# A two-layer hybrid trunk with eight experts: gate and up of the last third in one unit, and one activation table for logarithm and exponential

## The chip, the core and the metric

The kernel runs on one core of a Trainium2 chip. The metric is the device time of one execution in microseconds; lower is better. The core has five engines with queues of their own: TensorE (PE: matrix products, with its weight loads PEld beside them), VectorE (DVE), ScalarE (ACT), GpSimd (POOL) and SyncE (SP, which here only issues DMAs). They meet at semaphores: an instruction waits until a counter has reached a value, and each engine works strictly in the order in which its program is written.

## The reference

One inference step over 256 prompt tokens and 64 sample tokens (8 sequences of 8), width 1024. Layer 0 is a mixer of retention and mLSTM heads and a dense SwiGLU; layer 1 is the HGRN2 recurrence and a layer of eight experts of which each token takes two. The two parts that the change touches, cut to what is computed:

```python
def _hgrn2(q, k, log_f, v, S):              # 8 heads, in chunks; A = cumulative sum of log_f
    inter = einsum(qc * exp(A), S)
    dec   = exp(where(causal, A[t] - A[s], -inf))
    s     = einsum(qc, dec * kc)
    S_new = exp(A_end) * S + einsum(kc * exp(A_end - A), vc)
...
def _moe(h, ...):
    for e in range(8):
        out += gates[e] * (silu(h @ wg[e]) * (h @ wu[e])) @ wd[e]    # wg, wu: 1024x2816, wd: 2816x1024
```

f = lower + (1 - lower) * sigmoid(...), k = 1 - f, log_f = log(f), q = silu(...), all in float32.

## The kernel before, in words

**Products in three parts.** Every float32 weight is split into a high part (fp32r, written by ACT: `w_hi` L1716, `dense_hi` L1374) and a low part (the rest, written by DVE: `w_lo` L2361, `dense_lo` L1878). A product is three matmuls, high by high, low by high and high by low (`product3`, L509 to L511).

**The expert loop** (from 740 us of the span to its end) has eight rounds of one expert here, with up to 128 tokens each (`expert_round`). The 2816 hidden columns are taken in three chunks, c = 0, 1, 2, of 1024, 1024 and 768 columns. A round has 35 units of weights, in the order of `UNITS`: gate 0, up 0, gate 1, up 1, down 0, gate 2, up 2, down 1, down 2. A unit of gate or up holds two k-tiles of 128 rows (2x1024 columns, or 2x768 in chunk 2), one of down two rows of tiles. SP loads a unit into one of seven stages as soon as DVE has split what lay there (`load_unit`, L1279 and L1287); ACT and DVE split it into one of four slots as soon as PE has used what lay there (`SLOT_OF`, `ahead`). So PE is followed by ACT, ACT by DVE and DVE by SP, each at a fixed distance. A PSUM bank holds 512 columns: gate goes to banks 0 and 1, up to banks 2 and 3, and with 768 columns the second bank of each pair is half used: its matmuls have 256 columns. After the last unit of gate, ACT takes silu of it (`silu`, L1757); after the last unit of up, DVE multiplies (`product`, L2461); PE turns the result two units later (`turn`, L1151), and down needs it turned. `spread` (L1090) gathers the tokens of the next expert through banks 0 and 1.

The last round differs: at unit 20 DVE computes gates and slots first (`gates_and_last_slots`, L2433 to L2449), and the end of it is joined with the final norm.

**The third block** (HGRN2, 486 to 690 us) is an order written out by hand, `C_STEPS`, in which every engine picks the steps that concern it. Heads 0 to 3 are the first group (steps with a), heads 4 to 7 the second (b). f, q, g, v are tiles of the input projection on PE (L509 to L511), scaled to SBUF by DVE (L2290) or, for v, by ACT (L1662). sig, forget, ln make the forget gate on ACT (L1667, L1625/L1628, L1672), scan is its cumulative sum on DVE (L2297/L2298). For each of eight levels, da/db are differences on DVE (L2227/L2229), xa/xb their exponentials on ACT (L1634/L1637 for level 7, L1642, L1644), pa/pb products on DVE (L2237/L2238 for level 7, L2241/L2243), la/lb products on PE (L987, level 7 L982, the diagonal L966) that DVE takes over (L2258). wh and wl split the next dense unit (ACT L1374, DVE L1878). silu1 is silu of q of heads 4 to 7 (L1675). end, xend and kend (DVE L2323, ACT L1687 to L1690, DVE L2329) make the keys for the new state, which PE turns (turn, L720). ACT holds one table of functions at a time; where the next function is not in it, an ACT_TABLE_LOAD stands ahead of it.

Of the kernel before, what the change touches and what calls it, by code (L numbers as in the profile page):

```python
# [15 lines left out]
P = 128  # L16
# [55 lines left out]
    q4 sig1 pa5 forget4 la5 q5 forget5 xa6 la6 wh forget6 forget7 pa6 ln1 da7 scan1 xa7 q6 q7 wl la7 pa7 silu1 end0  # L72
    xend0 kend0 v0 xb0 v1 pb0 wh db1 wh xb1 wl lb0 turn0 lb1 v2 la8 v3 db2 pb1 v4 wl wh xb2 wl out0 v5 v6 pb2
# [97 lines left out]
def trunk_kernel(nc, A, O):  # L171
    with ExitStack() as ctx:
# [122 lines left out]
        part_units = lambda kind, c: [(kind, c, q) for q in range(CHW[c] // 256 if kind == "d" else KD // 2)]  # L295
        UNITS = [u for kind, c in (("g", 0), ("u", 0), ("g", 1), ("u", 1), ("d", 0), ("g", 2), ("u", 2), ("d", 1), ("d", 2))
# [4 lines left out]
        gate_end = {turn_of[("g", c, KD // 2 - 1)]: c for c in range(NCH)}  # L301
        up_end = {turn_of[("u", c, KD // 2 - 1)]: c for c in range(NCH)}
# [172 lines left out]
        def _(pe):  # L475
# [652 lines left out]
            def expert_round(it, last):  # L1128
# [18 lines left out]

                def turn(c):
# [47 lines left out]
                for p, (kind, c, q) in enumerate(UNITS):  # L1196
                    if kind == "d" and c == 2 and last:
                        if q == 0:
                            last_down()
                    elif kind == "d":  # L1200
                        down(c, q)
                    else:
                        gate_or_up(kind, c, q)
# [21 lines left out]
        def _(sp):  # L1225
# [44 lines left out]
            def load_unit(e, p):  # L1270
# [9 lines left out]
                else:  # L1280
                    n = CHW[c]
                    v = stage[:, 0:2 * n].rearrange("p (k n) -> p k n", n=n)
                    for j in range(2):
                        k = 2 * q + j
                        src = (wg if kind == "g" else wu)[:, bass.ds(e, 1), k:k + 1, c * CH:c * CH + n].rearrange(
# [48 lines left out]
        def _(act):  # L1334
# [295 lines left out]
            def level_exps(s, j):  # L1630
                act.wait_ge(S(f"level_diff{s}"), 8 - j)
                L = LV[s][j % 2]
                if j == 7:
                    fn(L[:, :, L_SECOND], CUM[:, 4 * s:4 * s + 4, P:TP], ACT.Exp)  # L1634
# [11 lines left out]
            for name, u in C_STEPS:  # L1646
# [18 lines left out]
                elif name == "sig":  # L1665
                    after_empty(act, ("c", "f", 7))
                    fn(K[:, 4:8, :], K[:, 4:8, :], ACT.Sigmoid).then_inc(S("f_sigmoid"), 1)  # L1667
                elif name == "forget":
# [170 lines left out]
        def _(dve):  # L1839
# [392 lines left out]
            def level_products(s, j):  # L2232
                L, at = LV[s][j % 2], slice(4 * s, 4 * s + 4)
                dve.wait_ge(S("hgrn_k"), 4 * s + 4)
                dve.wait_ge(S(f"level_exp{s}"), 8 - j)
                if j == 7:
                    v.tensor_tensor(L[:, :, L_SECOND], L[:, :, L_SECOND], Q[:, at, P:TP], ALU.mult)  # L2237
                    v.tensor_tensor(L[:, :, L_FIRST], L[:, :, L_FIRST], K[:, at, 0:P], ALU.mult).then_inc(S(f"level_mul{s}"), 1)  # L2238
# [45 lines left out]
            for name, u in C_STEPS:  # L2284
# [41 lines left out]
                elif name == "kend":  # L2326
                    at = slice(4 * u, 4 * u + 4)
                    dve.wait_ge(S("end_exp"), 2 * u + 2)
                    v.tensor_tensor(K[:, at, :], K[:, at, :], LV[u][1][:, :, :], ALU.mult).then_inc(S("hgrn_kend"), 1)  # L2329
# [121 lines left out]
            def expert_round(it, last):  # L2451

                def product(c):
# [6 lines left out]
                    for g, at in bank_columns(c):  # L2460
# [233 lines left out]
```

## Time and profile before

| what | us |
|---|---|
| median of three runs | 1516.8 (1511.55 to 1517.97) |
| the profiled execution | 1510.73 |
| its span, first to last instruction | 1508.9 |
| PE busy | 1479.9 (98%) |
| DVE busy | 1157.2 (77%) |
| ACT busy | 936.5 (62%) |
| the expert loop, from 740 to the end | 769 |

The span is what the trace covers; the 1.8 us beside it lie outside its first and last instruction. Busy time of PE counts matmuls that overlap (one of 512 columns is shown with 390 ns, and the next starts 227 ns after it), so PE's pace is read from the distance of starts, and its idle time from the bracket behind a row.

### The profile page before, as it was taken

What the parts mean: (1) busy time and instruction counts of PE and PEld (TensorE: products, weight loads), DVE (VectorE), ACT (ScalarE), POOL (GpSimd) and SP (SyncE); (2) the same over time, 40 slices, a digit from 0 to 9 for tenths busy, and PEclk for the clock granted to TensorE, in tenths of its full rate; (3) what the DMA queues carried; (4) which work ended last, traced back from release to release, by engine and by line L of the source; (5) the groups of instructions that cost most, each with busy time, mean ns of one, the idle gap of its engine ahead of it and who ended that gap; (6) DMA issues with size and microseconds to landing.
All of it is one profiled execution on the core that took longest, in us unless ns stands there. A gap on an engine that the chain in (4) does not pass through costs nothing.

```text
span 1508.9 us, 23251 instructions
## 1 busy us (share of the span) xinstructions
PE 1479.9 (98%) x8573; PEld 1312.6 (87%) x8573; DVE 1157.2 (77%) x1306; ACT 936.5 (62%) x975; POOL 88.3 (6%) x96
## 2 busy tenths in 40 slices
PE   9999999999999989999999999999999999999997
PEld 8899888999999979989788888888888888888885
DVE  5756677555455697777798888988889888898897
ACT  5434555334333774354777877778777787777875
POOL 1023110000000000120300000000000000000011
PEclk9999999999999999999999999999999999999999
DMA  8577724997445523451999999999999999999994
GB/s 250 134 136 139 138 88 135 284 296 208 123 145 175 159 84 114 144 159 60 362 406 381 389 362 394 378 377 385 363 393 380 377 389 358 391 379 379 395 334 170
DMA packets 213588, 404.03 MB, mean 268 GB/s; under 512 B 13471, under 2 KB 130491, under 8 KB 213390
## 3 DMA queue, kind: packets, MB, share of 16 engines
q1 hardware_dynamic: 202976, 372.82, 71.0%
q0 software_dynamic: 6320, 22.20, 4.9%
q10 hardware_dynamic: 4222, 8.05, 1.4%
q8 instruction: 47, 0.77, 0.2%
q14 instruction: 23, 0.19, 0.0%
HBM read 372.74 MB, written 30.28 MB: 267 GB/s over the span
## 4 chain that ended last, share of the span: by engine, by line
PE 87%; DVE 6%; ACT 3%; DMA 2%; issue 1%; POOL 0%; SPq 0%; DVEq 0%; ACTq 0%; POOLq 0%
PE bank L509 26%; PE bank L510 25%; PE bank L511 25%; PE bank L733 1%; DVE dense_lo L1878 1%; PE bank L1151 1%; DMA arena<-in_w_moe_down 1%; PE bank L775 1%; PE bank L678 1%; DVE w_lo L2361 1%; DVE arena L2007 1%; PE bank L725 1%; ACT dense_hi L1374 0%; PE bank L987 0%; PE bank L1100 0%
## 5 line engine op out<-in xcount | busy, mean ns | idle before, releaser
L2361 DVE TENSOR_TENSOR w_lo<-arena,w_hi 128x2048 fp32r<-128x2048 f32 (+1 forms) x280 | 596.9, 2165 | 87.1 <-ACT w_hi L1716 85.9
L1716 ACT ACTIVATE w_hi<-arena 128x2048 fp32r<-128x2048 f32 (+1 forms) x280 | 501.2, 1819 | 119.7 <-PE bank L511 114.2
L509 PE MATMUL bank<-w_hi,xg_hi 128*128 128x512 f32 (+1 forms) x768 | 287.3, 374 | 0.3
L510 PE MATMUL bank<-w_lo,xg_hi 128*128 128x512 f32 (+1 forms) x768 | 286.1, 373 | 0.0
L511 PE MATMUL bank<-w_hi,xg_lo 128*128 128x512 f32 (+1 forms) x768 | 285.4, 372 | 0.0
L1878 DVE TENSOR_TENSOR dense_lo<-ring,dense_hi 128x2048 fp32r<-128x2048 f32 (+1 forms) x78 | 167.8, 2151 | 122.0 <-ACT dense_hi L1374 121.9
L1374 ACT ACTIVATE dense_hi<-ring 128x2048 fp32r<-128x2048 f32 (+1 forms) x78 | 140.5, 1802 | 139.9 <-PE bank L511 114.7
L509 PEld LDWEIGHTS bank<-w_hi,xg_hi 128*128 128x128 f32 x768 | 144.5, 188 | 29.0 <-issue 3.1
L511 PEld LDWEIGHTS bank<-w_hi,xg_lo 128*128 128x128 f32 x768 | 144.2, 188 | 25.8
L510 PEld LDWEIGHTS bank<-w_lo,xg_hi 128*128 128x128 f32 x768 | 144.5, 188 | 24.9
L509 PE MATMUL bank<-h_hi,dense_hi 128*128 128x320 f32 x448 | 143.3, 320 | 3.9 <-DVE h_lo_a L1891 1.4
L509 PE MATMUL bank<-w_hi,at_hi 128*128 128x512 f32 x352 | 139.5, 396 | 0.2 <-DVE w_lo L2361 0.2
L511 PE MATMUL bank<-h_hi,dense_lo 128*128 128x320 f32 x448 | 139.3, 311 | 0.0
L511 PE MATMUL bank<-w_hi,at_lo 128*128 128x512 f32 x352 | 137.3, 390 | 0.0
L510 PE MATMUL bank<-w_lo,at_hi 128*128 128x512 f32 x352 | 137.0, 389 | 0.0
L509 PE MATMUL bank<-h_hi_f,dense_hi 128*128 128x320 f32 x352 | 109.0, 310 | 0.0
L510 PE MATMUL bank<-h_lo_f,dense_hi 128*128 128x320 f32 x352 | 108.8, 309 | 0.0
L511 PE MATMUL bank<-h_hi_f,dense_lo 128*128 128x320 f32 x352 | 108.8, 309 | 0.0
L509 PEld LDWEIGHTS bank<-h_hi,dense_hi 128*128 128x128 f32 x448 | 85.2, 190 | 8.0 <-DVE dense_lo L1878 3.2
L511 PEld LDWEIGHTS bank<-h_hi,dense_lo 128*128 128x128 f32 x448 | 85.0, 190 | 0.0
L510 PE MATMUL bank<-h_lo_a,dense_hi 128*128 128x320 f32 x256 | 79.3, 310 | 0.0
L511 PEld LDWEIGHTS bank<-w_hi,at_lo 128*128 128x128 f32 x352 | 66.1, 188 | 14.1
(458 smaller groups left out, 2383.2 us busy)
## 6 DMA issues: line engine op xcount, KB each, us to landing
arena<-in_w_moe_down SPq DMA_DIRECT2D x176, 512.0 KB, 6.7
arena<-in_w_moe_gate SPq DMA_DIRECT2D x128, 512.0 KB, 7.0
arena<-in_w_moe_up SPq DMA_DIRECT2D x128, 512.0 KB, 7.2
arena<-in_w_moe_gate SPq DMA_DIRECT2D x64, 384.0 KB, 5.7
arena<-in_w_moe_up SPq DMA_DIRECT2D x64, 384.0 KB, 4.1
ring<-in_w_in_ab SPq DMA_DIRECT2D x32, 512.0 KB, 9.2
ring<-in_w_in_c SPq DMA_DIRECT2D x32, 512.0 KB, 4.7
expert_rows<-ZERO SPq DMA_DIRECT2D x12, 1024.0 KB, 7.7
```

The costliest lines, as they stand in the source:

```text
L509: mm(out, left[0], right[0], start=start, stop=False)
L510: mm(out, left[0], right[1], start=False, stop=False)
L511: return mm(out, left[1], right[0], start=False, stop=stop)
L678: mm(banks[3][:, 0:256], ZERO[:, 0:P], ZERO[:, :], start=True, stop=True)
L725: mm(b[:, 0:TP], left(0), probs[:, 0:TP], start=True, stop=False, skip_group_check=True)
L733: ins = mm(b[:, TP + s * TS:TP + (s + 1) * TS], states[:, s, :], right[:, s * TS:(s + 1) * TS], start=False, stop=(s == NB - 1), skip_grou ...
L775: ins = mm(b[:, h * 256:(h + 1) * 256].rearrange("p (b v) -> p b v", v=DH), kn[rows_g, 2, :], VX[rows_g, at, :], start=True, stop=True)
L1151: ins = nc.tensor.transpose(banks[6 + j // 4][:, j % 4 * P:(j % 4 + 1) * P], AN[:, j * P:(j + 1) * P], ident)
L1374: fn(unit_flat(n, DWH), unit_flat(n, DST), ACT.Copy).then_inc(S("dense_hi"), 1)
L1716: fn(WH[SLOT_OF[p]][:, 0:unit_size(p)], STAGE[:, s, 0:unit_size(p)], ACT.Copy).then_inc(S("unit_hi"), 1)
L1878: v.tensor_tensor(unit_flat(n, DWL), unit_flat(n, DST), unit_flat(n, DWH).bitcast(F32), ALU.subtract).then_inc(S("dense_split"), 1)
L2361: v.tensor_tensor(WL[w][:, 0:n], STAGE[:, s, 0:n], WH[w][:, 0:n].bitcast(F32), ALU.subtract).then_inc(S("unit_split"), 1)
```

## The change

**In the expert loop**, chunk 2 has eight units of kind "gu" in place of four of gate and four of up: each holds one k-tile of gate (768 columns) and the same of up (768), side by side, 1536 columns as before. PE multiplies the 1536 columns in three pieces of 512, into banks 0, 1 and 2; bank 1 so holds the last 256 columns of gate and the first 256 of up. silu of chunk 2 comes after the last of these units instead of after the fourth, and DVE's product reads up from the second half of bank 1 and from bank 2. SP loads gate and up in turns.

**In the third block**, the table that holds both logarithm and exponential is asked for ahead of xa0 and behind sig1; level 7 signals after its first exponential as well, and DVE starts the first of its two products then. The steps at the first group's end stand in another order, end0 ahead of pa7, xb0 ahead of xend0 and pb0 ahead of kend0.

```diff
-    q4 sig1 pa5 forget4 la5 q5 forget5 xa6 la6 wh forget6 forget7 pa6 ln1 da7 scan1 xa7 q6 q7 wl la7 pa7 silu1 end0
-    xend0 kend0 v0 xb0 v1 pb0 wh db1 wh xb1 wl lb0 turn0 lb1 v2 la8 v3 db2 pb1 v4 wl wh xb2 wl out0 v5 v6 pb2
+    q4 sig1 pa5 forget4 la5 q5 forget5 xa6 la6 wh forget6 forget7 pa6 ln1 da7 scan1 xa7 q6 q7 wl la7 end0 silu1 xb0 pa7 pb0
+    xend0 kend0 v0 v1 wh db1 wh xb1 wl lb0 turn0 lb1 v2 la8 v3 db2 pb1 v4 wl wh xb2 wl out0 v5 v6 pb2
...
-        part_units = lambda kind, c: [(kind, c, q) for q in range(CHW[c] // 256 if kind == "d" else KD // 2)]
-        UNITS = [u for kind, c in (("g", 0), ("u", 0), ("g", 1), ("u", 1), ("d", 0), ("g", 2), ("u", 2), ("d", 1), ("d", 2))
+        part_units = lambda kind, c: [(kind, c, q) for q in range({"d": CHW[c] // 256, "gu": KD}.get(kind, KD // 2))]
+        UNITS = [u for kind, c in (("g", 0), ("u", 0), ("g", 1), ("u", 1), ("d", 0), ("gu", 2), ("d", 1), ("d", 2))
...
+                def gate_and_up(q):
+                    p = turn_of[("gu", 2, q)]
+                    pe.wait_ge(S("unit_split"), it * NU + p + 1)
+                    if q == 0:
+                        pe.wait_ge(S("silu_done"), it * NCH + 2)
+                        pe.wait_ge(S("a_ready"), it * NCH + 2)
+                    for g in range(3):
+                        at = slice(g * 512, (g + 1) * 512)
+                        ins = product3(banks[g][:, :], (XGH[:, q, :], XGL[:, q, :]),
+                                       [w[SLOT_OF[p]][:, at] for w in (WH, WL)], q == 0, q == KD - 1)
+                    ins.then_inc(S("unit_used"), 1)
...
-                        k = 2 * q + j
-                        src = (wg if kind == "g" else wu)[:, bass.ds(e, 1), k:k + 1, c * CH:c * CH + n].rearrange(
+                        k = q if kind == "gu" else 2 * q + j
+                        src = ((wg, wu)[j] if kind == "gu" else wg if kind == "g" else wu)[:, bass.ds(e, 1), k:k + 1, c * CH:c * CH + n].rearrange(
...
                 if j == 7:
-                    fn(L[:, :, L_SECOND], CUM[:, 4 * s:4 * s + 4, P:TP], ACT.Exp)
+                    if s == 0:
+                        nc.scalar.preload_act_table_set("natural_log_exp_and_others")
+                    fn(L[:, :, L_SECOND], CUM[:, 4 * s:4 * s + 4, P:TP], ACT.Exp).then_inc(S(f"level_exp{s}"), 1)
...
                     fn(K[:, 4:8, :], K[:, 4:8, :], ACT.Sigmoid).then_inc(S("f_sigmoid"), 1)
+                    nc.scalar.preload_act_table_set("natural_log_exp_and_others")
...
-                dve.wait_ge(S(f"level_exp{s}"), 8 - j)
+                dve.wait_ge(S(f"level_exp{s}"), 1 if j == 7 else 9 - j)
                 if j == 7:
                     v.tensor_tensor(L[:, :, L_SECOND], L[:, :, L_SECOND], Q[:, at, P:TP], ALU.mult)
+                    dve.wait_ge(S(f"level_exp{s}"), 2)
...
                     dve.wait_ge(S("end_exp"), 2 * u + 2)
+                    dve.wait_ge(S(f"level_mul{u}"), 8)
...
-                    for g, at in bank_columns(c):
-                        ins = v.tensor_tensor(AN[:, at], SL[:, at], banks[2 + g][:, 0:at.stop - at.start], ALU.mult)
+                    if c < 2:
+                        ups = [(at, banks[2 + g][:, 0:at.stop - at.start]) for g, at in bank_columns(c)]
+                    else:
+                        ups = [(slice(0, 256), banks[1][:, 256:512]), (slice(256, 768), banks[2][:, :])]
+                    for at, up in ups:
+                        ins = v.tensor_tensor(AN[:, at], SL[:, at], up, ALU.mult)
```

PE's program in the expert loop, first k-tiles of chunk 2 (w_hi_62 and w_lo_66 are parts of one slot of the weights, xg_hi and xg_lo the tokens; one bank of 512 columns is filled by three rows). Before:

```order
L509 MATMUL bank<-w_hi_62,xg_hi 128x512
L510 MATMUL bank<-w_lo_66,xg_hi 128x512
L511 MATMUL bank<-w_hi_62,xg_lo 128x512
L509 MATMUL bank<-w_hi_62,xg_hi 128x256
L510 MATMUL bank<-w_lo_66,xg_hi 128x256
L511 MATMUL bank<-w_hi_62,xg_lo 128x256
```

and in the changed kernel:

```order
L1150 REGISTER_ALU
L509 MATMUL bank<-w_hi_62,xg_hi 128x512
L510 MATMUL bank<-w_lo_66,xg_hi 128x512
L511 MATMUL bank<-w_hi_62,xg_lo 128x512
L509 MATMUL bank<-w_hi_62,xg_hi 128x512
L510 MATMUL bank<-w_lo_66,xg_hi 128x512
L511 MATMUL bank<-w_hi_62,xg_lo 128x512
```

The six rows before stand 16 times in a round (96 matmuls); in the changed kernel a k-tile of gate and up together has nine of 512 columns, 72 in a round.

ACT's program in the third block, from ln1 on. L1672 is the logarithm, L1644 xa7, L1675 silu1, L1687 the start of xend0. Before:

```order
L1672 ACT_TABLE_LOAD
L1672 ACTIVATE arena<-arena 128x1280
L1644 ACT_TABLE_LOAD
L1644 ACTIVATE arena<-arena 128x1280
L1675 ACT_TABLE_LOAD
L1675 ACTIVATE arena<-arena 128x1280
L1687 ACT_TABLE_LOAD
L1687 ACTIVATE arena<-arena,TOTAL 128x128
```

and in the changed kernel, where the same functions have the lines L1689, L1660, L1692 and L1704 and xb0 has L1650 and L1653:

```order
L1689 ACTIVATE arena<-arena 128x1280
L1660 ACTIVATE arena<-arena 128x1280
L1692 ACT_TABLE_LOAD
L1692 ACTIVATE arena<-arena 128x1280
L1650 ACT_TABLE_LOAD
L1650 ACTIVATE arena<-arena 128x4x128
L1653 ACTIVATE arena<-arena 128x128 x4
L1704 ACTIVATE arena<-arena,TOTAL 128x128
```

The loads ahead of the logarithm and of xa7 are gone (one that stood ahead of xa6 now stands right behind sig1), and xb0 is done ahead of xend0.

ACT's program in the expert loop at the end of chunk 2 (the register instructions between are the loop's counters). Before, silu of chunk 2 (L1757) stands two splits behind the start of up; in the changed kernel (L1774) it stands behind the split of unit 30:

```order
L1733 ACTIVATE w_hi_64<-arena 128x2048
L1768 REGISTER_ALU
L1774 ACTIVATE arena<-bank 128x512
L1774 ACTIVATE arena<-bank 128x256
L1732 REGISTER_ALU
L1733 ACTIVATE w_hi_62<-arena 128x2048
```

## Rows read from the trace of the kernel before

**Rows 1.** Busy time by stretch: us, PE, PEld, DVE, ACT, POOL, clock, DMA share, GB/s.

```profile
836.00:932.00 96.00, 95.98 (x461) 80.26 (x460) 82.80 (x50) 74.37 (x55) 0.00 (x0) 1.00 0.99 382
```

**Rows 2.** Waits of PE, 480 to 740 us: in total, times, longest.

```profile
PE bank L987 <- DVE arena L2243: 4.0, 3, 1.6
```

**Rows 3.** Waits of PE, 740 to 1508 us.

```profile
PE bank L509 <- DVE w_lo L2361: 0.2, 1, 0.2
```

**Rows 4.** Waits of the DMA queue, 836 to 1412 us.

```profile
SPq L1287 <- DVE w_lo L2361: 245.0, 141, 3.5
```

**Rows 5.** Timeline of PE, round 2: start, us, row, [idle before <-releaser].

```profile
862.49 0.48 PE L509 MATMUL bank<-w_hi,xg_hi 128*128 128x512 f32 x1
...
878.90 0.39 PE L509 MATMUL bank<-w_hi,at_hi 128*128 128x512 f32 x1
...
890.71 0.39 PE L509 MATMUL bank<-w_hi,xg_hi 128*128 128x512 f32 x1
...
906.09 0.28 PE L509 MATMUL bank<-w_hi,xg_hi 128*128 128x256 f32 x1
...
906.44 0.40 PE L509 MATMUL bank<-w_hi,xg_hi 128*128 128x512 f32 x1
...
907.49 0.40 PE L509 MATMUL bank<-w_hi,at_hi 128*128 128x512 f32 x1
```

**Rows 6.** Timelines around the end of chunk 2; the last row from round 8.

```profile
909.99 1.01 DVE L2461 TENSOR_TENSOR arena<-arena,bank 128x512 f32<-128x512 f32 x2
...
910.43 3.72 ACT L1716 ACTIVATE w_hi<-arena 128x2048 fp32r<-128x2048 f32 x2 [2.92 <-PE bank L511]
...
912.96 0.81 PE L1151 MATMUL bank<-cst,arena 128*128 128x128 f32 x6
...
1463.08 0.87 ACT L1757 ACTIVATE arena<-bank 128x512 f32<-128x512 f32 x2 [0.60 <-PE bank L511]
```

**Rows 7.** Last round: DVE's timeline, the chain's DMA, PE's timeline.

```profile
1461.33 13.37 DVE L2361 TENSOR_TENSOR w_lo<-arena,w_hi 128x1536 fp32r<-128x1536 f32 x7
...
1468.78 15.45 DMA arena<-in_w_moe_down
...
1488.62 0.50 PE L509 MATMUL bank<-w_hi,at_hi 128*128 128x512 f32 x1 [0.17 <-DVE w_lo L2361]
```

**Rows 8.** Timelines of ACT, DVE and PE at level 7 of the first group.

```profile
523.37 1.26 ACT L1637 ACTIVATE arena<-arena 128x128 f32<-128x128 f32 x4
...
524.76 0.69 DVE L2237 TENSOR_TENSOR arena<-arena 128x512 f32<-128x512 f32 x1 [1.44 <-ACT arena L1637]
...
526.11 1.16 PE L982 MATMUL bank<-arena 128*128 128x128 f32 x8 [0.93 <-DVE arena L2238]
```

**Rows 9.** Timelines of ACT, DVE and PE around the first group's end.

```profile
556.48 1.28 ACT L1672 ACT_TABLE_LOAD   x1
557.77 1.27 ACT L1672 ACTIVATE arena<-arena 128x1280 f32<-128x1280 f32 x1
...
557.37 0.88 DVE L2229 TENSOR_TENSOR arena<-arena 128x256 f32<-128x256 f32 x2
...
559.08 0.56 DVE L2297 TENSOR_TENSOR_SCAN arena<-cst,arena 128x192 f32<-128x192 f32 x1 [0.84 <-ACT arena L1672]
...
565.50 0.39 PE L509 MATMUL bank<-dense_hi,h_hi 128*128 128x256 f32 x1 [2.39 <-DVE dense_lo L1878]
...
568.43 0.40 ACT L1687 ACTIVATE arena<-arena,TOTAL 128x128 f32<-128x128 f32 x1 [2.58 <-DVE arena L2323]
...
571.52 1.49 DVE L2329 TENSOR_TENSOR arena<-arena 128x1280 f32<-128x1280 f32 x1 [3.13 <-ACT cst L1690]
...
575.33 0.55 PE L720 MATMUL bank<-cst,arena 128*128 128x128 f32 x3
```

**Rows 10.** Busy time by stretch, columns as in rows 1.

```profile
540.00:543.00 3.00, 2.12 (x16) 2.12 (x17) 3.00 (x11) 0.84 (x2) 0.00 (x0) 1.00 0.01 2
...
566.00:570.00 4.00, 4.00 (x24) 4.00 (x23) 2.39 (x8) 1.57 (x6) 0.00 (x0) 0.57 0.80 266
```

More of the change, by code:

```diff
@@ L300, in trunk_kernel @@
         turn_of = {u: p for p, u in enumerate(UNITS)}
-        gate_end = {turn_of[("g", c, KD // 2 - 1)]: c for c in range(NCH)}
-        up_end = {turn_of[("u", c, KD // 2 - 1)]: c for c in range(NCH)}
+        gate_end = {turn_of[("g", c, KD // 2 - 1) if c < 2 else ("gu", 2, KD - 1)]: c for c in range(NCH)}
+        up_end = {turn_of[("u", c, KD // 2 - 1) if c < 2 else ("gu", 2, KD - 1)]: c for c in range(NCH)}
         gate_last, up_last = {c: p for p, c in gate_end.items()}, {c: p for p, c in up_end.items()}
@@ L1201, in expert_round @@
                         down(c, q)
+                    elif kind == "gu":
+                        gate_and_up(q)
                     else:
```

## The prediction

> **What bounds the kernel now.** I read the busy times by stretch first, then who waited for whom, then the timelines where the change sits. In the expert loop PE is busy 95.98 of 96 us at a clock of 1.00 [rows 1], and from 740 us on it waits for weights once, 0.2 us [rows 3]. The DMA engines look full as well, 0.99 [rows 1], but their queue waited 245 us in 576 for DVE to free a stage [rows 4], for one of its two lines alone: transfers follow PE, not the other way round. So a round ends when PE has got through its matmuls. The last round is different (below). In the third block PE does wait: 4.0 us for DVE's level products [rows 2] and 2.39 us at 565.50 for the low part of a dense unit [rows 9]. Those waits lie on the path, since PE has nothing else queued that could run.
>
> **The loop.** The row to compare is chunk 2, 890.71 to 907.49: 16.78 us for 96 matmuls [rows 5]. One k-tile of gate or of up is 906.44 to 907.49, 1.05 us, three matmuls of 512 columns and three of 256. The three of 256 take 906.09 to 906.44, 0.35 us; so the three of 512 take 0.70 us, 0.233 each. The changed stretch is 72 matmuls of 512 columns. A stretch of just that is in the same round, 862.49 to 878.90: 16.41 us [rows 5], 0.228 each. The saving is 16.78 - 16.41 = 0.37 us a round. From one side it is bounded by the case that the 512s keep 0.233: 72 x 0.233 = 16.8, nothing saved. From the other: the stretch of 16.41 starts behind transposes and its first row is 0.48 us long instead of the usual 0.39 [rows 5]; without that 0.09 us it is 16.32, and the saving 0.46. I take 0.37, since that is the same instruction in the same number.
>
> The Trainium skill ("TensorE: Matmul & The Clock Gate", Back-to-back issue gap) has a lone matmul's gap at its columns over 2.4 GHz plus about 2.5 ns. By that rule, as an estimate, 24 fewer matmuls save 24 x 2.5 ns = 0.06 us a round. The trace has 0.117 us for 256 columns and 0.228 for 512 and no such constant; I follow the trace, and keep the rule's outcome as a rival.
>
> The saving counts in seven rounds, not eight. In the last round DVE splits seven units back to back from 1461.33 for 13.37 us, behind its work on gates and slots; the last unit's transfer is issued at 1468.78 off that chain, lands 15.45 us later, and PE waits for its low part at 1488.62 [rows 7]. That chain starts from units before chunk 2, so PE reaches the wait earlier and waits longer. 7 x 0.37 = 2.6 us.
>
> What hides the rest: silu of chunk 2 moves behind the eighth unit. PE ends that at 907.49, and ACT sat idle for 2.92 us until 910.43 there [rows 6]; silu of 768 columns takes 0.87 (the row of round 8). DVE starts its product at 909.99, which was later than PE because it still split, and PE turns at 912.96. silu done at about 908.6 is ahead of 909.99, so the product doesn't move; its cover is 912.96 - 911.00 = 1.96 us, of which the faster PE takes 0.37 at most. Queued behind silu on ACT are the splits of units 31 and 32, which wait for PE until 910.43 anyway. The moved loads are as many, of the same size and in the same stages, and the bytes are the same; only their order changes. The required rate rises by 0.4%. I cost both at nothing.
>
> **The third block, level 7.** ACT's single exponential of the second half ends as the four others start, 523.37; they last 1.26; DVE idled 1.44 us until 524.76 and then did two products, and PE had waited 0.93 us at 526.11 [rows 8]. Now the first product (0.69) runs beside the four exponentials, and only the second lies behind them: PE starts some 0.6 us earlier, and so does everything on DVE, which has no gap from there to the differences that feed xa5 and whose chain then runs over ACT. I take 0.6; bounds are 0 (a tile of PE becomes late in that stretch, where its clock is low for a while) and 0.69.
>
> **ln1 and xa7.** The load at 556.48 lasts 1.28; the logarithm follows at 557.77, and DVE, free at 557.37 + 0.88 = 558.25, waits 0.84 us for it until 559.08 [rows 9]. The load that stood ahead of xa6 still costs its 1.28 in the same gap, only earlier. Without the load of ln1, the logarithm ends at 557.77 and is no longer late; DVE's differences are what is late next, so the scan gains 0.84 and not 1.28. Then come the scan, q6, q7 and the split for v0, in an unbroken row on DVE, and PE's wait of 2.39 us before 565.50 [rows 9] ends 0.8 us earlier. With the 0.6, PE starts v0 at 564.1. The second load removed, ahead of xa7, lies beside DVE's scan: nothing.
>
> In the new order xend0 waits for xb0. Before, ACT was ready for xend0 2.58 us ahead of 568.43 [rows 9], at 565.85; silu1 and its loads ahead of that follow q7 on DVE, so they come 1.4 us earlier, 564.4. xb0 takes 1.26 for its four exponentials [rows 8] and some 0.5 for the one before them: xend0 starts at 566.2 instead of 568.43, and kend0 at 571.52 - 2.2 = 569.3, for 1.49 us. PE wants it for turn0, 575.33 - 565.50 = 9.8 us behind v0's start: at 573.9, or 572.3 if the clock stays up. Cover at the least 572.3 - 570.8 = 1.5 us. DVE idled 3.13 us ahead of kend0 [rows 9]; of that the earlier start takes 0.8 and pb0's two products (0.69 each, [rows 8]) 1.4. No new wait.
>
> **The clock.** Behind the 2.39 us gap PE's granted clock was 0.57 on average from 566 to 570, that is, mostly at 1.2 instead of 2.4 GHz [rows 10], which costs 4 x 0.43 = 1.7 us, all of it on PE's path. Behind a gap of near 0.9 us within 540 to 543 the clock stayed at 1.00 [rows 10], and PE's longest wait for L2243 was 1.6 us [rows 2]. The new gap is 2.39 - 0.8 = 1.6 us. Whether the clock falls after it can't be told from one trace; I take it that it does not, with 6 in 10, and count 0 to 1.7.
>
> **The sum.** Loop 2.6, level 7 0.6, ln1 0.8, clock 1.7: 5.7 us; 4.0 if the clock still falls. Against the profiled execution, 1510.73 (span 1508.9 and 1.8 beside it), that is 1505.0. The runs shown have a median of 1516.8, 6.1 above the profiled one; carried over to it, 1516.8 - 5.7 = 1511.1. The runs spread over 6.4 us (1511.55 to 1517.97), more than the change, so a median of the changed kernel can fall at either side of that: 1506 or 1512.
>
> **Rivals.**
> 1. The clock falls as before, and the rest holds: 4.0 us, 1512.8. For it: the gap only shrinks, it doesn't go. Against it: the gap of 1.6 us.
> 2. The loop gives nothing, because the 512s keep 0.233 or because the gap is as the rule has it; the block gives 1.4 and perhaps 1.7: 1516.8 - 1.4 to 3.1, 1514. For it: the wide 512s in rows 5. Against it: no other stretch of only 512s runs at 0.233.
> 3. PE gets more than I count: 0.46 in eight rounds (3.7), and the waits for L2243 shrink too, since ACT is 1.3 us freer. 3.7 + 1.4 + 1.7 + 1.5 = 8.3: 1508.5.
> 4. Slower. The product of chunk 2 comes late. Its cover is 1.96 us [rows 6]; if silu misses ACT's idle 2.92 us and falls behind the next two splits (3.72 us, from 910.43), it ends at 915.0 and the product at 916.0, 3.1 us behind the turn. In seven rounds 21 us, less the 5.7: 1532. It decides from the point where silu ends later than about 912. Against it: in ACT's program silu stands ahead of those splits.
>
> That the table change does nothing is excluded by ACT's program: the two loads are gone from it.
>
> **How the numbers follow.** Forecast 0.50, rival 1 0.22, rival 2 0.13, rival 3 0.11, rival 4 0.04. A difference under 0.5% (7.6 us) can't be told from none here. Faster by more is rival 3 and those cases of the forecast and of rival 1 in which the median falls among the lower runs, 0.11 + 0.20: 0.31. Slower by more is rival 4: 0.04. The rest, 0.65, is within. The range: low from 1506 less a margin for rival 3, 1504.5; high from rival 2 with the spread of a median, 1516.5. It leaves out rival 4 and the outer parts of 2 and 3.
>
> **What would show it.** Right: chunk 2 of rounds 1 to 7 takes 16.4 us, the last unit's wait in round 8 grows by about 0.4, and PE waits for no product; PE's wait before v0 is 1.6 us, the one at level 7's product 0.3, the clock stays at 1.00 behind v0's start; ACT has no load between xa6 and silu1. Wrong: 16.8 us in chunk 2, a bracket on PE's L1163 (turn) or on its L720, or a span that falls by more than 7 us.

## The result and the profile after

| | before | after |
|---|---|---|
| first comparison, median (lowest to highest), 5 runs each | 1516.27 (1511.55 to 1517.97) | 1503.42 (1500.85 to 1505.5) |
| ratio, 95% interval | | 0.9932 (0.9905 to 0.9958) |
| second comparison, later runs (experiment 1), 12 and 7 runs | 1510.05 (1508.61 to 1518.96) | 1504.06 (1501.99 to 1504.5) |
| ratio, 95% interval | | 0.9954 (0.9937 to 0.9972) |
| profiled execution (span) | 1510.73 (1508.9) | 1504.12 (1502.3) |

The changed kernel is faster. 1503.42 lies 7.7 us under the forecast of 1511.1 and 1.1 under the low end of the range. The two profiles lie 6.6 us apart and the second comparison 6.0; the forecast difference was 5.7. So the change is worth about 6 us, and what failed is how it was carried over to a median (the section on why the prediction was right and wrong). A ratio is estimated over all runs of a comparison and differs a little from the quotient of the two medians.

The lines of the changed kernel (the run "after"): chunk 2 of gate and up is L509 to L511 as before, turn is L1163, the splits are L1733 (high) and L2380 (low), silu L1774, product L2484. In the block the logarithm is L1689, the scan L2315, silu1 L1692, xend L1704, kend L2348, the low part of a dense unit L1895, level products L2254 to L2261.

Expert loop: PE's timeline in round 2 of after, to be read against [rows 5]:

```profile
859.49 0.48 PE L509 MATMUL bank<-w_hi,xg_hi 128*128 128x512 f32 x1
...
875.91 0.39 PE L509 MATMUL bank<-w_hi,at_hi 128*128 128x512 f32 x1
...
887.72 0.39 PE L509 MATMUL bank<-w_hi,xg_hi 128*128 128x512 f32 x1
...
904.04 0.39 PE L509 MATMUL bank<-w_hi,at_hi 128*128 128x512 f32 x1
```

Chunk 2 takes 904.04 - 887.72 = 16.32 us (16.78 before), the stretch that I took as its model still 16.42. All rounds 1 to 7 together took 657.53 us and now take 654.20. Around the end of chunk 2, against [rows 6]:

```profile
904.24 0.87 ACT L1774 ACTIVATE arena<-bank 128x512 f32<-128x512 f32 x2
906.68 1.01 DVE L2484 TENSOR_TENSOR arena<-arena,bank 128x256 f32<-128x256 f32 x2
906.96 3.72 ACT L1733 ACTIVATE w_hi<-arena 128x2048 fp32r<-128x2048 f32 x2 [1.85 <-PE bank L511]
...
909.48 0.82 PE L1163 MATMUL bank<-cst,arena 128*128 128x128 f32 x6
```

silu sits in ACT's gap (2.92 us of idle time became 1.85), ends at 905.1, and the product still ends 1.8 us before PE's turn, which has no bracket. PE's waits from 737 us of after to the end, against [rows 3]:

```profile
PE bank L1121 <- ACT last_hi L1844: 1.2, 1, 1.2
PE bank L509 <- DVE w_lo L2380: 0.3, 1, 0.3
```

The first is in the tail (before has it too), the second in the last round, right behind DVE's work on gates.

Third block, level 7 of the first group (ACT, DVE, PE), against [rows 8]:

```profile
522.19 1.26 ACT L1653 ACTIVATE arena<-arena 128x128 f32<-128x128 f32 x4
522.41 0.69 DVE L2254 TENSOR_TENSOR arena<-arena 128x512 f32<-128x512 f32 x1 [0.28 <-ACT arena L1650]
...
523.48 0.69 DVE L2256 TENSOR_TENSOR arena<-arena 128x512 f32<-128x512 f32 x1 [0.38 <-ACT arena L1653]
...
524.23 0.94 PE L982 MATMUL bank<-arena 128*128 128x128 f32 x6 [0.23 <-DVE arena L2256]
```

DVE's first product now runs beside the four exponentials, and PE waits 0.23 us instead of 0.93. From the logarithm to turn0, in order of time, against [rows 9]:

```profile
554.48 1.28 ACT L1689 ACTIVATE arena<-arena 128x1280 f32<-128x1280 f32 x1
...
556.30 0.54 DVE L2315 TENSOR_TENSOR_SCAN arena<-cst,arena 128x192 f32<-128x192 f32 x1
...
560.48 1.27 ACT L1692 ACTIVATE arena<-arena 128x1280 f32<-128x1280 f32 x1 [1.50 <-DVE arena L2308]
...
562.70 0.39 PE L509 MATMUL bank<-dense_hi,h_hi 128*128 128x256 f32 x1 [1.47 <-DVE dense_lo L1895]
...
564.77 0.39 ACT L1704 ACTIVATE arena<-arena,TOTAL 128x128 f32<-128x128 f32 x1
...
567.85 1.49 DVE L2348 TENSOR_TENSOR arena<-arena 128x1280 f32<-128x1280 f32 x1 [1.05 <-ACT cst L1707]
...
571.04 0.55 PE L720 MATMUL bank<-cst,arena 128*128 128x128 f32 x3
```

The scan has no bracket (0.84 before), PE's wait ahead of v0 is 1.47 (2.39 before), kend ends 1.7 us before turn0, and turn0 waits for nothing. The granted clock behind v0 and later in the block (the third number from the end of a row), against [rows 10]:

```profile
562.00:566.00 4.00, 3.30 (x27) 3.30 (x28) 4.00 (x10) 3.99 (x11) 0.00 (x0) 1.00 0.54 169
566.00:570.00 4.00, 4.00 (x36) 4.00 (x35) 2.94 (x6) 3.36 (x10) 0.00 (x0) 1.00 0.29 98
656.00:663.00 7.00, 7.00 (x25) 3.90 (x26) 5.37 (x11) 3.62 (x7) 2.12 (x3) 0.51 0.60 204
```

Behind v0 it stays at the upper level, 2.4 GHz, where before had 0.57 for 4 us. But from 656 to 663 us it is at the lower level of 1.2 GHz, with PE busy all the time before (36.00 of 36 us from 620 to 656) and in it; in the same stretch before had 1.00. Where the 6.6 us between the two profiles went, by distances of starts on PE:

| stretch | before | after | change |
|---|---|---|---|
| start to level 7's first product, without its wait | 525.18 | 524.00 | -1.2, unchanged code |
| PE's wait at that product | 0.93 | 0.23 | -0.7 |
| that product to v0 | 39.39 | 38.47 | -0.9 |
| v0 to the loop | 174.92 | 175.20 | +0.3 |
| rounds 1 to 7 | 657.53 | 654.20 | -3.3 |
| last round, to the last product with the gathered rows | 100.77 | 100.04 | -0.7 |
| from there to the end | 10.18 | 10.16 | 0.0 |

The first line isn't the change's: before has a clock fall at 208 to 211 us (0.50 there) that after doesn't have, in code that is the same. Without that line 5.4 us are left. The second pair of profiles (before_again, 1507.45, and after_again, 1503.67) lies only 3.8 us apart, because there the unchanged stretch ahead of level 7 is 1.9 us longer in the changed kernel; without it 5.7 are left.

### The profile page after: what moved, and what is told of

Read it like the earlier page. It is cut to its first block, busy times and chain, and to the rows that moved or that the text cites. A ratio compares the mean times of both kernels' runs of the same rounds, so it can differ in the third digit from the quotient of the medians.

```text
span 1502.3 us, 22859 instructions
## 1 busy us (share of the span) xinstructions
PE 1475.0 (98%) x8381; PEld 1300.3 (87%) x8381; DVE 1156.2 (77%) x1306; ACT 935.7 (62%) x973; POOL 89.5 (6%) x96
## 4 chain that ended last, share of the span: by engine, by line
PE 91%; DVE 7%; ACT 2%; issue 1%; POOL 0%; DVEq 0%; ACTq 0%; POOLq 0%
PE bank L509 27%; PE bank L511 26%; PE bank L510 26%; PE bank L733 2%; DVE dense_lo L1895 1%; PE bank L1163 1%; PE bank L775 1%; PE bank L678 1%; PE bank L657 1%; PE bank L987 1%; PE bank L725 1%; PE bank L1100 0%; PE bank L666 0%; PE bank L1090 0%; DVE arena L2024 0%
## 5 line engine op out<-in xcount | busy, mean ns | idle before, releaser
L2380 DVE TENSOR_TENSOR w_lo<-arena,w_hi 128x2048 fp32r<-128x2048 f32 (+1 forms) x280 | 596.9, 2165 | 82.1 <-ACT w_hi L1733 80.0
L1733 ACT ACTIVATE w_hi<-arena 128x2048 fp32r<-128x2048 f32 (+1 forms) x280 | 502.0, 1820 | 117.0 <-PE bank L511 111.1
L509 PE MATMUL bank<-w_hi,xg_hi 128*128 128x512 f32 x704 | 275.6, 392 | 0.5 <-DVE w_lo L2380 0.3
L511 PE MATMUL bank<-w_hi,xg_lo 128*128 128x512 f32 x704 | 274.1, 389 | 0.0
L510 PE MATMUL bank<-w_lo,xg_hi 128*128 128x512 f32 x704 | 273.9, 389 | 0.0
L1895 DVE TENSOR_TENSOR dense_lo<-ring,dense_hi 128x2048 fp32r<-128x2048 f32 (+1 forms) x78 | 167.8, 2151 | 122.5 <-ACT dense_hi L1388 122.3
L509 PEld LDWEIGHTS bank<-w_hi,xg_hi 128*128 128x128 f32 x704 | 132.1, 188 | 30.7 <-issue 3.1
L511 PEld LDWEIGHTS bank<-w_hi,xg_lo 128*128 128x128 f32 x704 | 132.1, 188 | 27.7
L510 PEld LDWEIGHTS bank<-w_lo,xg_hi 128*128 128x128 f32 x704 | 132.2, 188 | 27.0
L509 PE MATMUL bank<-h_hi,dense_hi 128*128 128x320 f32 x448 | 142.2, 317 | 3.9 <-DVE h_lo_a L1908 1.4
L509 PE MATMUL bank<-w_hi,at_hi 128*128 128x512 f32 x352 | 139.3, 396 | 0.0
L511 PE MATMUL bank<-h_hi,dense_lo 128*128 128x320 f32 x448 | 138.3, 309 | 0.0
L511 PE MATMUL bank<-w_hi,at_lo 128*128 128x512 f32 x352 | 137.3, 390 | 0.0
L509 PE MATMUL bank<-h_hi_f,dense_hi 128*128 128x320 f32 x352 | 109.0, 310 | 0.0
L511 PE MATMUL bank<-h_hi_f,dense_lo 128*128 128x320 f32 x352 | 108.8, 309 | 0.0
L509 PEld LDWEIGHTS bank<-h_hi,dense_hi 128*128 128x128 f32 x448 | 84.2, 188 | 8.0 <-DVE dense_lo L1895 3.2
L511 PEld LDWEIGHTS bank<-h_hi,dense_lo 128*128 128x128 f32 x448 | 84.1, 188 | 0.0
L511 PEld LDWEIGHTS bank<-w_hi,at_lo 128*128 128x128 f32 x352 | 66.1, 188 | 14.0
```

What stands on the lines that cost most here:

```text
L509: mm(out, left[0], right[0], start=start, stop=False)
L510: mm(out, left[0], right[1], start=False, stop=False)
L511: return mm(out, left[1], right[0], start=False, stop=stop)
L1733: fn(WH[SLOT_OF[p]][:, 0:unit_size(p)], STAGE[:, s, 0:unit_size(p)], ACT.Copy).then_inc(S("unit_hi"), 1)
L1895: v.tensor_tensor(unit_flat(n, DWL), unit_flat(n, DST), unit_flat(n, DWH).bitcast(F32), ALU.subtract).then_inc(S("dense_split"), 1)
L2380: v.tensor_tensor(WL[w][:, 0:n], STAGE[:, s, 0:n], WH[w][:, 0:n].bitcast(F32), ALU.subtract).then_inc(S("unit_split"), 1)
```

## The experiments

**1. How far do two copies of one kernel lie apart?** No edit.

> An unchanged copy of the kernel before, for a second profile and to see how far two of its medians lie apart. The plain runs of before and after lie 12.8 us apart in their medians, the two profiles 6.6. Theory A (two levels of the kernel before: its runs lie near 1512 or near 1517, by how often TensorE's clock falls): the runs of this copy fall near both levels, the ratio's interval holds 1, and a run at 1517 has a mean clock lower by about 0.003 than one at 1512. Theory B (it waits for DMAs in some runs): the clock is the same in long and short runs, and the profile shows other waits of PE for transfers. In the last round PE's first matmul on the last unit of down waits 0.17 us for its low part again if that wait belongs to the schedule; with a transfer of another length than 15.45 us it is chance.

1508.52 us (11 runs) beside 1510.17 (35 runs of the kernel before), ratio 0.9992 (0.9981 to 1.0003). Theory A holds in part: long runs exist, but they are rare. Of 47 runs of the kernel before in this study's two timed comparisons, 42 lie between 1507.7 and 1511.8 and 5 between 1515.0 and 1520.7; none of the copy's 11 is of the long kind. Three of the five long runs have a mean clock of 0.988 to 0.990, below all others (0.992 to 0.996); the other two, at 0.992 and 0.993, can't be told from them by the clock. In the first comparison 3 of 5 were of the long kind. The last round shows what was chance in the profile of before. Its last down transfer was issued at 1468.78 us, and ACT began to split it at 1484.33, 15.55 us later; in before_again the issue was at 1466.01 and the split began 12.64 us later, in after at 1462.92 and 13.82 us later. The rows of the split, in this order:

```profile
1484.33 1.91 ACT L1716 ACTIVATE w_hi<-arena 128x2048 fp32r<-128x2048 f32 x1 [3.13 <-DMA arena<-in_w_moe_down]
```

```profile
1478.65 1.92 ACT L1716 ACTIVATE w_hi<-arena 128x2048 fp32r<-128x2048 f32 x1 [0.57 <-DMA arena<-in_w_moe_down]
```

```profile
1476.73 1.91 ACT L1733 ACTIVATE w_hi<-arena 128x2048 fp32r<-128x2048 f32 x1 [1.95 <-DMA arena<-in_w_moe_down]
```

In the 14 profiles this distance is 11.8 to 14.0 us, but for before (15.55) and tables_again (18.29, below). The 18 matmuls around the wait of [rows 7] (1485.45 to 1490.12 us of before) take 4.67 us there and 4.18 to 4.20 in all other profiles but tables_again.

> An unchanged copy of the changed kernel, timed beside runs of the kernel before on the same chip. In the first comparison the medians lay 12.8 us apart; alone, the loop's part gave 2.9 us and the block's part 2.7 us against one and the same set of runs. Theory A (the parts add, and the first comparison met a slow group of the kernel before): 1504 to 1505 against 1510, a difference of 5 to 6 us, ratio 0.9965. Theory B (both together give more than their sum): 10 us or more, ratio 0.993 again. In the trace: level 7's first product to v0 takes 38.5 us, rounds 93.49 us, the last round 100.0 us to the last down matmul, and the clock is at 1.00 behind v0.

1504.06 against 1510.05, ratio 0.9954 (0.9937 to 0.9972). Theory A: the difference is 6.0 us. The trace has 38.48 us from level 7 to v0, 654.18 for seven rounds, 100.36 for the last round (the wait behind the gates was 0.58 us here).

**2. Each half alone.** loop_only has the change's edits of the expert loop (the units of kind "gu" and what follows from them) and the third block as before. block_only has the edits of the third block (both preloads, level 7's early signal, the order of the steps with kend's wait) and the loop as before.

> Only the change in the expert loop (units of gate and up together in chunk 2), the third block as before. My theory: the loop's part is 7 times 0.46 us plus what the last round gives, 3.3 to 4.1 us, and chunk 2 takes 16.3 us; nothing changes ahead of the loop. So about 1511 to 1512 against a kernel before at 1515, ratio 0.9975. Rival (the two parts help each other, or the loop's part is worth more in plain runs than in the profile): 8 us or more. Rival (the gain came with the block's other clock phase): chunk 2 at 16.8.

1507.30 against 1510.17 (-2.9), ratio 0.9989 (0.9974 to 1.0004); chunk 2 16.32 us, seven rounds 654.26, last round 100.06. The interval holds 1 (two of its 12 runs are of the long kind), so it's the rows of the trace that show the loop's part, not the runs.

> Only the change in the third block, the loop as before. My theory: 0.7 us at level 7, 0.9 us ahead of v0, and the clock behind v0 stays at 1.00, 1.5 us, which a clock fall later can give back: 1.6 to 3.1 us, ratio 0.9985. Chunk 2 takes 16.78 us. Rival (the clock): the plain runs gain more than 5 us, because the kernel before loses more to clock falls in its runs than in its profile, and the mean clock listed with the runs is higher by 0.002 or more than that of the runs before.

1507.46 (-2.7), ratio 0.9987 (0.9978 to 0.9996); level 7's wait 0.23, 38.46 us to v0, seven rounds 657.55. -2.9 and -2.7 add up to -5.6, and both together gave -6.0: the halves add up as far as the runs can tell, and neither holds a hidden 10 us.

**3. Widths or units?**

```diff
-                    for g in range(3):
-                        at = slice(g * 512, (g + 1) * 512)
+                    for g, (a0, a1) in enumerate(((0, 512), (512, 768), (768, 1280), (1280, 1536))):
```

> The loop's change as in loop_only (eight units of gate and up together, silu behind the last, same loads), but each k-tile is multiplied in pieces of 512, 256, 512 and 256 columns as before, 96 matmuls in chunk 2. If the gain comes from the widths alone, chunk 2 takes 16.78 us and the kernel is the same as before (ratio 1.000). If it comes from the units' order, the loads' order or silu's place, chunk 2 takes 16.3 us and the ratio is 0.9975.

1510.75, ratio 1.0007 (0.9989 to 1.0026). PE's timeline, first and last row of chunk 2 and the first of down: 908.05 - 891.27 = 16.78 us. Seven rounds take 657.55 us (657.53 before), the last 100.31.

```profile
891.27 0.39 PE L509 MATMUL bank<-w_hi,xg_hi 128*128 128x512 f32 x1
...
907.93 0.28 PE L511 MATMUL bank<-w_hi,xg_lo 128*128 128x256 f32 x1
908.05 0.40 PE L509 MATMUL bank<-w_hi,at_hi 128*128 128x512 f32 x1
```

The loop's gain is the widths of PE's matmuls; units, loads and silu's place are worth nothing either way in the trace (by the runs alone, nothing to within 4 us). Then the same columns in six pieces of 256 (`for g in range(6)` over 256 columns each):

> As loop_only, but the 1536 columns of a k-tile are multiplied in six pieces of 256: 144 matmuls in chunk 2 instead of 72. Theory of a fixed cost for each matmul (24 fewer saved 0.46 us, so 19 ns each, and 256 columns cost 0.123 us): 144 x 0.123 = 17.7 us for chunk 2. Theory of the change of width (256 columns cost 0.1167 us as their three rows in the trace show, and it is a 512 next to a 256 that costs 0.233 instead of 0.227): 144 x 0.1167 = 16.8 us.

One profile. Its chunk 2 begins and ends like this:

```profile
888.93 0.28 PE L1159 MATMUL bank<-w_hi,xg_hi 128*128 128x256 f32 x1
889.05 0.28 PE L1160 MATMUL bank<-w_lo,xg_hi 128*128 128x256 f32 x1
...
906.09 0.28 PE L1161 MATMUL bank<-w_hi,xg_lo 128*128 128x256 f32 x1
906.21 0.40 PE L509 MATMUL bank<-w_hi,at_hi 128*128 128x512 f32 x1
```

17.28 us for 144, 0.120 each: between the two theories, so both were half right. 512 columns cost 16.32 / 72 = 0.2267 us, 256 cost 0.1200: the second 256 columns add 0.1067 us, which is their number over 2.4 GHz, and 13 ns are left for each matmul at either width. A third width checks it. Two rows of after's dense tiles of 320 columns, 15 matmuls apart:

```profile
527.71 0.31 PE L511 MATMUL bank<-h_hi,dense_lo 128*128 128x320 f32 x1
...
529.91 0.31 PE L511 MATMUL bank<-h_hi,dense_lo 128*128 128x320 f32 x1
```

2.20 / 15 = 0.1467 us, and 320 / 2.4 GHz + 13 ns is 0.1463. So 24 fewer matmuls save 24 x 13 ns = 0.32 us of the 0.46. The other 0.14 come with the change of width: 48 x 0.2267 + 48 x 0.1200 = 16.64, and the mixed stretch takes 16.78.

The 13 ns are measured with weights of 128 columns and aren't a constant of every such matmul. after_again has matmuls of 256 columns with weights of 64 columns and, right behind them, with 128 (first and last row of each):

```profile
586.15 0.28 PE L511 MATMUL bank<-dense_hi,h_lo_c 128*64 128x256 f32 x1
...
588.54 0.28 PE L511 MATMUL bank<-dense_hi,h_lo_c 128*64 128x256 f32 x1
...
588.89 0.28 PE L511 MATMUL bank<-dense_hi,h_lo_c 128*128 128x256 f32 x1
...
591.29 0.28 PE L510 MATMUL bank<-dense_lo,h_hi 128*128 128x256 f32 x1
```

2.39 us for 21 is 0.1138 each, 7 ns beside the columns; 2.40 for 20 is 0.1200 again. Matmuls of 320 columns with weights of 36 (level7_only, L511 at 35.96 to L511 at 39.00 us) are 3.04 us for 21, 0.1448 each, 11 ns. What sets this cost isn't shown.

**4. The block's three edits, one at a time.** tables_only has the two preloads alone:

```diff
+                    if s == 0:
+                        nc.scalar.preload_act_table_set("natural_log_exp_and_others")
...
+                    nc.scalar.preload_act_table_set("natural_log_exp_and_others")
```

> The kernel before with one edit: the table with logarithm and exponential is asked for ahead of xa0 and behind sig1. Level 7 and the order of the steps stay. My theory: the scan no longer waits 0.84 us for the logarithm, PE's wait ahead of v0 is 2.39 - 0.84 = 1.55 us and the clock stays at 1.00 from there on; PE's wait at level 7 stays at 0.93. Rival (DVE was late anyway): the wait ahead of v0 stays near 2.4 and the clock falls.

Level 7 to v0 took 38.47 us (39.39 to 39.41 in six profiles without the tables; loop_only, below, aside), PE's wait there 1.47, no clock fall behind. The run as a whole took 1518.04, and its windows show why:

```profile
113.00:131.00 18.00, 16.58 (x71) 15.40 (x71) 5.93 (x14) 3.15 (x9) 1.55 (x3) 0.53 0.44 96
```

18 us at a mean clock of 0.53, in code that no kernel here changes: up to 8.5 us lost (18 x 0.47). It is the one long run that was profiled.

> A second profile of tables_only, whose first one had a clock fall of 17 us at 114 to 131 us, far ahead of the block. My theory: that fall is chance and is gone, level 7's first product is at 524 to 526 us instead of 533.6; its distance to v0 is 38.5 us again, with a wait of 1.47 us and a clock of 1.00 behind it. From v0 to the loop's start 173.6 us if no clock fall follows, 175 to 176 if one does near 660 us. Rival (the fall at 114 belongs to this kernel): it is there again.

The early fall is gone (level 7 at 523.97); 38.45 us to v0 again. This run has two other things. Its last down transfer took 18.19 us to land (by the chain of work that ended last), PE waited 2.9 us for it, and the last round took 105.18 us, so a late last transfer, as in [rows 7], isn't bound to one execution (tables_again has the loop of before; no profile of the changed loop has one). And PE waited at the second group's level 7, as it did in tables_only (0.62):

```profile
571.94 1.16 PE L982 MATMUL bank<-arena 128*128 128x128 f32 x8 [0.63 <-DVE arena L2241]
```

The same row of after, where xb0 and pb0 come ahead of xend0 and kend0, has no bracket:

```profile
571.43 1.06 PE L982 MATMUL bank<-arena 128*128 128x128 f32 x8
```

Level 7's early signal alone:

```diff
-                    fn(L[:, :, L_SECOND], CUM[:, 4 * s:4 * s + 4, P:TP], ACT.Exp)
+                    fn(L[:, :, L_SECOND], CUM[:, 4 * s:4 * s + 4, P:TP], ACT.Exp).then_inc(S(f"level_exp{s}"), 1)
...
-                dve.wait_ge(S(f"level_exp{s}"), 8 - j)
+                dve.wait_ge(S(f"level_exp{s}"), 1 if j == 7 else 9 - j)
...
+                    dve.wait_ge(S(f"level_exp{s}"), 2)
```

> The kernel before with one edit: level 7 signals after its first exponential, and DVE starts its first product then. My theory: PE's wait at its first product of level 7 falls from 0.93 to about 0.25 us; the wait ahead of v0 stays at 2.4 us and the clock falls behind it to about 0.57. Rival: a later tile of PE takes the 0.7 us up, and the distance from the start of the block to v0 doesn't change.

The first theory in each number: 0.23 us at level 7, then 39.41 us to v0 with its wait of 2.40, and a clock fall behind it.

The order alone (the two changed lines of `C_STEPS` and kend's wait for the level products):

> The kernel before with one edit: end0 ahead of pa7, xb0 ahead of xend0, pb0 ahead of kend0, and no change of tables or signals. My theory: it gives nothing, since no PE wait hangs on it: the wait ahead of v0 stays at 2.4 us, the clock falls as before, and the distance from v0 to the loop's start stays near 175 us. Rival (xb0 earlier lets lb0 and what follows start earlier, or pa7 later delays la7): PE's waits between la7 and lb1 change by more than 0.3 us.

Nothing: 39.40 us to v0, wait 2.39, clock fall behind it, 174.81 to the loop. What the order is for shows where the clock stays up behind v0. In the six profiles with the fall there, PE comes late to level 7 of the second group, and pb0 is in time in either order. Where the fall is missing, the three profiles with the old order have PE wait 0.62 to 0.63 us (tables_only, tables_again, and loop_only, whose wait ahead of v0 is the long one, 2.41 us), and the five with the new order don't have it wait. The wait is the same with and without the tables, so it's the clock that makes PE early, and then the old order takes 0.6 us back. The row of loop_only:

```profile
575.50 1.16 PE L982 MATMUL bank<-arena 128*128 128x128 f32 x8 [0.63 <-DVE arena L2252]
```

**5. Is the clock behind v0 a gain?**

> A second profile of block_only, for the clock behind v0. With the wait of 1.47 us ahead of v0 the three profiles so far had no clock fall there, with the wait of 2.4 us six of seven had one. If the clock's part is a real gain, v0 to the loop's start is 173.6 us again, about 1.3 us below the mean of the kernels with the long wait (174.9). If it is given back, a clock fall near 660 us of 7 us or so takes its place, and the distance is 175 or more, as in two of the three.

173.60 us, the same as block_only. Over all profiles of this case (fall: granted clock under 0.95 within 5 us behind v0):

| PE's wait ahead of v0 | profiles | with a fall behind v0 | v0 to the loop, us |
|---|---|---|---|
| 2.4 | 7 | 6 | 174.36 to 175.38, mean 174.86 |
| 1.47, the change's order of steps | 5 | 0 | 173.57 to 175.21, mean 173.92 |
| 1.47, the old order (tables_only, tables_again) | 2 | 0 | 176.12 and 175.39 |

The shorter wait does keep the clock up, 7 times of 7. The last line holds the 0.6 us of the old order, so what the change gets is read from the line above it: a mean gain of 0.9 us up to the loop, not 1.7. It is 1.3 us in four of the five (173.57 to 173.64), and in after it's turned over by a later fall. Such falls come near 660 us (one starts at 666): 7 us long in after, tables_only, tables_again and loop_only, the one profile of the upper row without a fall behind v0. Where v0's fall came, the one near 660 lasts 3.5 us or is missing. At half the clock a fall of 3.5 us can cost up to 1.7 us and one of 7 up to 3.4, less the waits that it hides: after_again has one of 3.5 us at 659 and takes 173.59 us, block_only has none, waits 1.39 us for a transfer instead and takes 173.57; with its 7 us, after takes 175.21.

**6. Is DVE the pace of this stretch?** The changed kernel with one copy moved from DVE to ACT:

```diff
-                    b = open_bank("dve")
+                    kind = "dve" if s else "act"
+                    b = open_bank(kind)
...
+                elif name == "la" and u == 1:
+                    b = take(("lv", 0, 7))
+                    free(fn(PH[:, 0:4, P:TP], b[:, :].rearrange("p (h n) -> p h n", n=P), ACT.Copy))
```

> The changed kernel with one more edit: the first copy of level scores of the first group (DVE, 0.67 us at 529.29 in the trace of the changed kernel) is done by ACT, which sat idle for 3.2 us there. DVE has no gap from 524 to 562 us in that trace, so my theory is that its work sets PE's pace in this stretch and each us taken from it is a us for PE: from PE's first product of level 7 to v0 37.8 instead of 38.5 us, PE's first wait for the level products 0.5 instead of 1.15, and 0.6 us less in all. Rival (ACT's exponentials or PE itself set the pace): 38.5 us as before. In the plain runs 0.6 us can't be told from nothing.

1502.73 us, ratio 0.9947 (0.9927 to 0.9967): the lowest median of all, not to be told from after's 0.9954. In the trace PE's first wait for the level products fell from 1.15 to 0.55 us, as DVE's chain has it, but from level 7 to v0 it took 38.58 us, not 37.8. A row of PE's timeline, a later one, and the clock between them:

```profile
530.40 1.16 PE L988 MATMUL bank<-arena 128*128 128x128 f32 x8 [0.55 <-DVE arena L2265]
...
544.52 1.16 PE L988 MATMUL bank<-arena 128*128 128x128 f32 x8 [0.23 <-DVE arena L2265]
```

```profile
538.00:542.00 4.00, 3.96 (x18) 3.96 (x19) 3.38 (x10) 1.30 (x2) 0.00 (x0) 0.57 0.00 0
```

The clock fell from 538 to 542, which after does not have; PE came late to 544.52, and DVE, which waits for PE's banks in turn, lost what it had gained. loop_only had the same at 541 to 545 (39.91 us to v0). The gain of a DVE instruction is real at the next wait, and this one profile can't show that it reaches v0.

## Why the prediction was right and where it was wrong

- **The carry-over to the median: wrong, and the cause of the miss.** "Carried over to it, 1516.8 - 5.7 = 1511.1." The three runs shown lay 6.1 us above the profiled one, and two of them were of the long kind that is 5 of 47 in later comparisons. I took a shift for a constant that is the share of runs with a long clock fall. From the profiled execution the same sum gave 1505.0, and after's medians were 1503.42 and 1504.06: 6.1 of the 7.7 us are this step; of the rest 0.3 are the sum's (below), and the others are within what medians and profiles of one kernel differ by. Why the first comparison met so many long runs stays open; that a long clock fall makes a long run is shown for one profile (tables_only), the mean clock tells it for three of five others, and for the other two it isn't shown.
- **Loop, 7 x 0.37 = 2.6: right mechanism, undersized.** It is 7 x 0.46 = 3.2 to 3.3 us. The upper bound in the text was the value: the model stretch of 16.41 starts with a row of 0.48 us because transposes stand ahead of it, and chunk 2 follows matmuls of 512. The text also read 0.117 us for 256 columns out of a stretch of mixed widths and saw "no such constant"; matmuls of 256 alone take 0.120, and there is one. The rule that I kept as a rival (the Trainium skill, "TensorE: Matmul & The Clock Gate", Back-to-back issue gap: for a lone matmul, about 2.5 ns beside the columns) would have had 24 x 2.5 ns = 0.06 us a round. These runs have 13 ns with fp32r operands and a weight load of 128 columns for each matmul, at three widths; here the measurement decides.
- **Last round, nothing: wrong by 0.2.** "PE reaches the wait earlier and waits longer." It rested on the transfer of [rows 7], which was late by chance: the last unit's wait of 0.17 us is in no other profile but tables_again's (2.9), and in after it's gone instead of 0.4 longer. What grows is another wait, the one behind the gates: 0.10 to 0.24 us with the old widths, 0.32 to 0.58 with the new. It takes back about half of the 0.46. The last round takes 100.28 to 100.41 us in seven profiles with the old widths and no late transfer, and 100.04 to 100.36 in four with the new, 0.2 us less in the mean. The 0.7 between the two profiles are this and the late transfer.
- **silu, product, order of the loads, nothing: right.** Experiment 3 prices them at zero.
- **Level 7, 0.6: right** (0.70; its upper bound 0.69). The rest of the block did not take it back.
- **ln1, 0.84: right** (0.93, by the distance to v0). The table ahead of xa7 was counted at nothing; no run has it alone, and at most the 0.09 left over are its.
- **xend0 and kend0: right.** Forecast 2.1 and 5.2 us behind v0, measured 2.07 and 5.15, DVE's idle time 1.05 (0.9 by the text). But the order of the steps has a worth that the text didn't count: with the clock up, the old order has PE wait 0.6 us at the second group's level 7.
- **The clock, 1.7 with 6 in 10: the fall went, about half of the gain came.** The step counted the clock behind v0 and stopped there. By v0 to the loop it is worth 0.9 us in the mean of the five profiles with the change's block, 1.3 in four and less than nothing in after. In rival 1 the gain was to fail because the clock falls as before; in after it failed because it falls later. One reading was off: the gap within 540 to 543 was taken as "near 0.9 us", but the stretch's edge had cut it. It's the wait of 1.59 us ahead of PE's row at 540.88, the 1.6 of [rows 2], as long as the gap forecast ahead of v0. The clock stayed at 1.00 behind it in before, but behind the same wait loop_only's fell (541 to 545), so one such place settles nothing. The row of before:

```profile
540.88 1.16 PE L987 MATMUL bank<-arena 128*128 128x128 f32 x8 [1.59 <-DVE arena L2243]
```

- **Rival 3** had the 0.46, and its other half was wrong: the waits for the level products (4.0 us in before) are 5.3 in before_again and in after, since a clock fall at 528 to 532 us hid 1.3 us of them in before. **Rival 2 and rival 4** are excluded by experiments 2 and 3 and by the turn without a bracket.

By the steps as measured: 0.7 + 0.9 + 3.3 + 0.2 + 0.9 = 6.0 us, against 6.0 by the medians (the ratio's interval, 0.9937 to 0.9972, is 4.2 to 9.5 us); that they agree to the tenth is luck, since the clock's part alone varies by 1.6 us from profile to profile. The forecast sum of 5.7 was near it partly by luck too: the clock was counted 0.8 too high, the loop with its last round 0.9 too low, and the block's two waits 0.2. On the bound of 0.5% the two comparisons fall on different sides, 0.68% and 0.46%, and both intervals hold it.

## What to carry to other kernels

Where PE sets the pace, count its matmuls as well as its columns: pieces that fill a bank, built across two operands if need be, save a cost each that a profile gives from two widths, each measured in a stretch of its own. A clock fall that an edit removes should be followed to the end of the stretch before it is booked, over several profiles, since it may come back a hundred us later. And a difference belongs on the profiled execution's own time; how far the median of three runs lies above that is chance. Two profiles of one kernel differ as well (1510.73 and 1507.45 for the kernel before), so compare them by stretches and leave out those that no edit touches.

## What the runs showed of the hardware that I had not expected

- An fp32r matmul with its own weight load of 128 columns costs 13 ns beside its columns at 2.4 GHz (0.1200 us for 256, 0.1467 for 320, 0.2267 for 512), with a load of 64 columns 7 ns (0.1138 for 256) and with one of 36 columns 11 ns (0.1448 for 320); and mixing 512 and 256 in threes costs 0.14 us more for 96 of them.
- PE's clock falls although PE is busy: near 660 us it is at 1.2 GHz for 3.5 or for 7 us in 11 of 14 profiles. In the three without it (before, order_only, block_only) PE waited 1.2 to 1.4 us for the state's transfer at 673 to 678 us instead. Near 730 us (741 in tables_only) it falls for 3.5 us in 10 of 14, and the four without have PE wait 0.62 us for the tokens' low part as the loop starts. The longest fall, 17 us at 114 to 131 us, began within a wait of 1.42 us for a transfer; order_only waited 1.19 us at the same place and had no fall.
